# The opening of every projection and MLP phase: the first weight slab in two halves, and PE's first pass outside its loop

## The reference

```python
for l in range(DEPTH):                      # 4 layers
    kind, j = l % N_MIXERS, l // N_MIXERS
    hp, hs = modulate(xp, mp[0], mp[1]), modulate(xs, ms[0], ms[1])
    if kind == 0:                           # layers 0 and 3: RWKV-7
        ...  # r, k, v = xr @ w_rkv[0], xk @ w_rkv[1], xv @ w_rkv[2]; scan; y @ w_o
    elif kind == 1:                         # layer 1: attention
        ...  # qkv = h @ w_qkv; attention; @ w_o
    else:                                   # layer 2: gated DeltaNet
        ...  # proj = h @ w_in; chunked delta rule; @ w_o
    xp = deepnorm_residual(xp, dp, mp[2], ln_g[l, 0], ln_b[l, 0])
    xs = deepnorm_residual(xs, ds, ms[2], ln_g[l, 0], ln_b[l, 0])
    # squared_relu_mlp(h, w_fc1, w_fc2) = square(relu(h @ w_fc1)) @ w_fc2, D_FF = 4096
    xp = deepnorm_residual(xp, squared_relu_mlp(modulate(xp, mp[3], mp[4]), w_fc1[l], w_fc2[l]), mp[5], ...)
    xs = deepnorm_residual(xs, squared_relu_mlp(modulate(xs, ms[3], ms[4]), w_fc1[l], w_fc2[l]), ms[5], ...)
```

## Time and profile before

| | |
|---|---|
| time, median of 3 runs | 6409.85 us (6405.69 to 6411.26) |
| time of the profiled execution | 6404.79 us |
| its span | 6402.7 us |
| PE busy | 5409.3 us (84%) in 66124 matmuls |
| DVE busy | 2506.2 us (39%) |
| ACT busy | 1872.1 us (29%) |
| DMA | 424.21 MB, a mean of 66 GB/s |

### The profile page before, as it was taken

How to read it: one execution, slowest core, us unless ns; L and a number is a source line. 1 busy time by engine, 2 the same in 40 slices (tenths; PEclk the granted TensorE clock), 3 DMA queues, 4 the chain that set the end, 5 groups by cost and what they waited for, 6 DMA issues and landing times. The chain is left out here.

```text
span 6402.7 us, 149362 instructions
## 1 busy us (share of the span) xinstructions
PE 5409.3 (84%) x66124; PEld 4859.5 (76%) x66124; DVE 2506.2 (39%) x4363; ACT 1872.1 (29%) x3847; POOL 586.3 (9%) x1076
## 2 busy tenths in 40 slices
PE   6678999978997487789978588789968899996998
PEld 2377888868996365689977577679948688885998
DVE  0233555434333522243331454343352355444433
ACT  1023334322222122322232343232222344333222
POOL 0002223200000000000000222000000232210000
PEclk8788999989998677899989799899989899997999
DMA  9621000012212100122122211122112100001221
GB/s 407 259 99 49 22 24 22 9 48 84 74 52 73 45 11 21 47 79 79 52 94 78 65 39 40 56 73 73 67 41 92 34 14 24 23 8 71 73 79 49
DMA packets 105057, 424.21 MB, mean 66 GB/s; under 512 B 19081, under 2 KB 34697, under 8 KB 73929
## 3 DMA queue, kind: packets, MB, share of 16 engines
q1 hardware_dynamic: 91280, 386.14, 17.1%
q10 hardware_dynamic: 13248, 30.15, 1.2%
HBM read 367.25 MB, written 49.26 MB: 65 GB/s over the span
## 5 line engine op out<-in xcount | busy, mean ns | idle before, releaser
L356 PE MATMUL bank<-src_hi,ring_hi 128*128 128x320 f32 x4032 | 937.1, 314 | 344.6 <-DVE ring_lo L348 336.0
L356 PEld LDWEIGHTS bank<-src_hi,ring_hi 128*128 128x128 f32 x4032 | 686.6, 192 | 343.6 <-issue 339.2
L356 PE MATMUL bank<-src_lo,ring_hi 128*128 128x320 f32 x4032 | 933.2, 313 | 0.0
L356 PE MATMUL bank<-src_hi,ring_lo 128*128 128x320 f32 x4032 | 931.0, 313 | 0.0
L356 PEld LDWEIGHTS bank<-src_lo,ring_hi 128*128 128x128 f32 x4032 | 687.2, 191 | 5.4 <-issue 5.4
L356 PEld LDWEIGHTS bank<-src_hi,ring_lo 128*128 128x128 f32 x4032 | 685.8, 191 | 0.0
L348 DVE TENSOR_TENSOR ring_lo<-ring,ring_hi 128x2048 fp32r<-128x2048 f32 x190 | 434.9, 2289 | 513.9 <-ACT ring_hi L344 513.0
L562 ACT ACTIVATE stage<-bank 128x320 f32<-128x320 f32 x512 | 196.1, 435 | 1409.4 <-PE bank L356 1409.4
L356 PE MATMUL bank<-hidden_hi,ring_hi 128*128 128x320 f32 x2048 | 467.2, 309 | 0.0
L356 PE MATMUL bank<-hidden_lo,ring_hi 128*128 128x320 f32 x2048 | 467.1, 309 | 0.0
L356 PE MATMUL bank<-hidden_hi,ring_lo 128*128 128x320 f32 x2048 | 467.0, 309 | 0.0
(11 more groups left out here) (361 smaller groups left out, 8673.2 us busy)
## 6 DMA issues: line engine op xcount, KB each, us to landing
ring<-w_mlp SPq DMA_DIRECT2D x128, 1024.0 KB, 4.8
mod_ring<-w_mod SPq DMA_DIRECT2D x48, 2048.0 KB, 12.1
ring<-rw_wrkv SPq DMA_DIRECT2D x24, 1024.0 KB, 4.9
ring<-dn_win SPq DMA_DIRECT2D x16, 1024.0 KB, 5.1
rkv<-stage ACTq DMA_DIRECT2D x48, 320.0 KB, 2.2
r_k<-rkv SPq DMA_DIRECT2D x32, 320.0 KB, 3.6
src<-mixed SPq DMA_DIRECT2D x32, 320.0 KB, 8.0
dn_proj<-stage ACTq DMA_DIRECT2D x32, 320.0 KB, 2.2
```

Of the source, the lines that this page charges most:

```text
L356: last = self.nc.tensor.matmul(acc[h][:, 0:HALF], wt[:, n % 2, k, m * P:(m + 1) * P], x[:, k, h * HALF:(h + 1) * HALF], start=first and q ...
```

## The change

The first slab of each of the sixteen phases is loaded, cast and subtracted in two halves: FRONT, its blocks k 0 to 3, and BACK, its blocks k 4 to 7. FRONT has three semaphores of its own. SP issues FRONT ahead of everything; with `load` one source block follows, then BACK, then the other seven source blocks. ACT and DVE do the two halves at places of their own among the source blocks. PE waits for FRONT before product 0 and for BACK before product 4. For these waits PE's pass 0 is written out ahead of the loop, which then runs from pass 1.

```diff
+    def load_first(self, sp, part):
+        done = self.s["w_half"] if part is FRONT else self.s["w_loaded"][0]
+        sp.dma_start(self.raw[:, 0, part].rearrange("p k n -> p (k n)"),
+                     slab(self.w, 0)[:, part.start * 2 * P:part.stop * 2 * P]).then_inc(done, 16)
+    def upper_first(self, act, part):
+        act.wait_ge(self.s["w_half"] if part is FRONT else self.s["w_loaded"][0], 16)
+        self.nc.scalar.copy(self.hi[:, 0, part], self.raw[:, 0, part]).then_inc(self.s["wh_half" if part is FRONT else "wh_ready"], 1)
...
 # projection, SP
+                ring.load_first(sp, FRONT)
                 if load is not None:
-                    for b in range(NB):
+                    sp.dma_start(src[:, 0, :], load[0]).then_inc(s["src_loaded"][0], 16)
+                ring.load_first(sp, BACK)
+                if load is not None:
+                    for b in range(1, NB):
                         sp.dma_start(src[:, b, :], load[b]).then_inc(s["src_loaded"][b], 16)
-                        if b == 1:
-                            ring.load(sp, 0, PER, 0)
-                else:
-                    ring.load(sp, 0, PER, 0)
                 ring.load(sp, 0, PER, 1)
 # projection, PE
-                with pe.Fori(0, n_pass) as i:
+                def block_(i, first):
                     for n in range(PER):
-                        pe.wait_ge(s["wl_ready"], at(i, PER, n + 3))
+                        if n or not first:
+                            pe.wait_ge(s["wl_ready"], at(i, PER, n + 3))
...
-                                if u == 0:
+                                if first and u == 0:
                                     pe.wait_ge(s["src_ready"], k + 1)
+                                    if k == FRONT.start:
+                                        pe.wait_ge(s["wl_half"], 1)
+                                    if k == BACK.start:
+                                        pe.wait_ge(s["wl_ready"], 3)
...
+                block_(0, True)
+                with pe.Fori(1, n_pass) as i:
+                    block_(i, False)
 # projection, ACT
+                    if load is not None and b == 0:
+                        ring.upper_first(act, FRONT)
...
-                    if b == 2:
-                        ring.upper(act, 0, PER, 0)
+                    if load is None and b == 2:
+                        ring.upper_first(act, FRONT)
+                    if b == (3 if load is None else 0):
+                        ring.upper_first(act, BACK)
 # projection, DVE
+                    if load is not None and b < 2:
+                        ring.rest_first(dve, (FRONT, BACK)[b])
...
-                    if b == 3:
-                        ring.rest(dve, 0, PER, 0)
+                    if load is None and b in (2, 3):
+                        ring.rest_first(dve, (FRONT, BACK)[b - 2])
 # mlp, ACT and DVE (SP and PE as above)
-                    if b == 2:
-                        ring.upper(act, 0, PER, 0)
+                    if b in (3, 4):
+                        ring.upper_first(act, (FRONT, BACK)[b - 3])
...
-                    if b == 3:
-                        ring.rest(dve, 0, PER, 0)
+                    if b in (3, 4):
+                        ring.rest_first(dve, (FRONT, BACK)[b - 3])
```

More of the change, by code:

```diff
@@ L312, in _ @@
             modulate_blocks(dve, nc, g, lambda b: None, mod_at(0, 1), mod_at(0, 0))
-SPLIT_SEMS = ["w_loaded:2", "wh_ready", "wl_ready", "mm_done", "evacuated", "hi_ready", "src_ready"]
+SPLIT_SEMS = ["w_loaded:2", "wh_ready", "wl_ready", "mm_done", "evacuated", "hi_ready", "src_ready", "w_half", "wh_half", "wl_half"]
+FRONT, BACK = slice(0, NB // 2), slice(NB // 2, NB)
 HALF = T // 2
@@ L338, in load, with rest_first @@
                      slab(self.w, i * per + n)).then_inc(self.s["w_loaded"][n % 2], 16)
+    def load_first(self, sp, part):
[5 more added lines that the diff above has]
+        self.nc.scalar.copy(self.hi[:, 0, part], self.raw[:, 0, part]).then_inc(self.s["wh_half" if part is FRONT else "wh_ready"], 1)
+    def rest_first(self, dve, part):
+        dve.wait_ge(self.s["wh_half" if part is FRONT else "wh_ready"], 1)
+        self.nc.vector.tensor_tensor(self.lo[:, 0, part], self.raw[:, 0, part], self.hi[:, 0, part].bitcast(F32),
+                                     ALU.subtract).then_inc(self.s["wl_half" if part is FRONT else "wl_ready"], 1)
     def upper(self, act, i, per, n):
@@ L516, in _ @@
             def _(sp):
-                with sp.Fori(0, QUARTERS) as i:
+                ring.load_first(sp, FRONT)
+                ring.load_first(sp, BACK)
+                for n in range(1, PER):
+                    ring.load(sp, 0, PER, n)
+                with sp.Fori(1, QUARTERS) as i:
                     for n in range(PER):
@@ L523, in _, with block_ @@
                 pe.sem_inc(s["mm_done"], 4)
-                with pe.Fori(0, QUARTERS) as i:
+                def block_(i, first):
                     for n in range(PER):
-                        pe.wait_ge(s["wl_ready"], at(i, PER, n + 3))
+                        if n or not first:
+                            pe.wait_ge(s["wl_ready"], at(i, PER, n + 3))
                         for m in range(2):
@@ L538, in _ @@
                             last.then_inc(s["mm_done"], 1)
+                block_(0, True)
+                with pe.Fori(1, QUARTERS) as i:
+                    block_(i, False)
             @block.scalar
```

## The result

The kernel after takes 6362.23 us (median of 4 runs, 6355.86 to 6366.58) against 6410.56 us before (4 runs beside them, 6405.69 to 6414.69). The ratio is 0.9925, with a 95% interval from 0.9913 to 0.9937: 48 us faster. The forecast was 6349, with a range from 6337 to 6372. The direction was right and the time inside the range, but 13 us above the middle, and a fifth of the expected gain did not come. The profiled execution took 6355.86 us, its span 6354.1 us against 6402.7.

The account below looks back on a forecast made before the run. PE bounds the projection and MLP phases, latency the rest. Gains of 28.6 + 28 - 4 + 8.6 - 0.4 = 60.8 us, taken from 6409.85, gave 6349 us, range 6337 to 6372.

Parts of the forecast that it names:

- Source in SBUF: `at_wqkv`, `dn_win` and four `mlp`: PE starts 4.7 or 4.8 us earlier and the phases keep it; 28.6 us together.
- Source by DMA: Four output products: unit 0's product 7 ends 7.3 us sooner in layer 0, 6.6 to 7.5 elsewhere; sum 28 us.
- clock rival: Where PE now pauses in unit 0, ten openings: clock stays at 0.50 longer, costing 20 to 28 us; 6372; chance 0.10.
- Source made by DVE: Six products with `mix`: PE starts sooner, but unit 0 waits for DVE's longer chain; a loss of 4 us.
- PE's pass outside the loop: The written-out first pass costs nothing itself but moves PE's loops; 8.6 us won in the third `mlp`, at 85%.
- the step on the third loop: Third `mlp`: its loop body moves 17 places, out of the bad ones, ending 8.6 us of branch stalls; 85%.
- The rival's 6355: Third `mlp` still misses, at two branches, giving back two thirds of 8.6 us; chance 0.10 together with all four missing.
- the prediction's two signs of being wrong: Granted clock in unit 0 stays at 0.50 beyond 7 us, or third `mlp`'s fetches continue after its loop's first pass.
- halves land together: A half takes a slab's 4.8 us: FRONT 1.2 us later in twelve openings, gain 15 us smaller; 6364; chance 0.06.
- The slower rival: All 16 openings: clock doesn't rise before unit 1 is through, 95 us lost less the 61; 6444; chance 0.02.

Follow-up runs that it names:

- The run with the 64 waits: The kernel after with 64 already-met PE waits ahead of the third `mlp`'s loop, moving it 32 places; 6341.92 us, ratio 0.9896.
- the kernel with 434 waits: The kernel after with 434 already-met PE waits ahead of the first `mlp`'s loop, moving every later PE instruction 217 places; one run, 6396.86 us.

## Why the prediction was right, and where it was wrong

**Source in SBUF: right in the start, and lucky in the total.** The start comes 4.3 to 4.9 us sooner in the six phases (forecast 4.7 and 4.8). FRONT lands 4.1 us after its issue in `at_wqkv` and the first `mlp`, not 3.6, and a half takes ACT 1.04 and DVE 1.23 us, not 0.95 and 1.14. An estimate by the Trainium skill's page "DMA: Bandwidth & Descriptors", section "Anatomy of one DMA", is 3.2 us for this half; the Trainium skill gives that formula for transfers issued by GpSimd, and these are issued by SP. The trace has 0.9 more, and the measurement decides. The end of unit 0 gained 4.3 to 5.7 us. In four of the six it gained more than the start, by 0.4 to 1.3 us, where the low clock was shorter than before (3.1 us in `at_wqkv`, before 6.0). With the third `mlp`'s opening the six give 31.2 us against 28.6. The starts alone give 27.6. The other 3.6 came from the clock and are in no term of the sum, so it was luck for the forecast that they made good what other terms lacked.

**Source by DMA: mechanism right, 3.7 us over.** Of these 3.7, 2.6 are the long execution in the table; by the means (297.6 us over the three kernels with the old opening, 270.8 over the five with the new one) the gain is 26.7 of 28. The pause after product 0 came, 0.4 to 1.1 us long where 1.3 was forecast for layer 0. Two terms were mis-sized: FRONT landed 4.7 us after its issue in layer 0 and not 3.6, so the start was 7.9 us behind the first issue and not 6.8; and the clock, taken to rise as in a dense opening, stayed low for 8.0 to 9.3 us in three of four. This is the clock rival in a small form, in four openings and not in ten. With `mix` the pauses come later, and the low stretch was 3.2 to 5.9 us, within the 3.2 to 6.1 of the openings before (the prediction read them as 3.4 to 6.2).

**Source made by DVE: right.** Forecast -4, measured -3.8, by the steps given: PE starts earlier, DVE's chain is longer, and the pauses come from product 3 on. The whole slab in the kernel after, at 407.00 us, confirms the sign. It is also 2.9 us below the kernel before, where two slabs had landed late (the prediction has 5.6 and 6.4 us for them). That the size fits so closely is partly chance: three kernels with the old opening took 407.4 to 409.9 us, and by their mean, 408.6, the loss is 5.2.

**PE's pass outside the loop: the peel is free, but the step on the third loop failed.** The step said that the third body stood at most 20 places short of a good one, from the fourth body that was fine 20 places further on, and that 17 of the 20 take it out, at 85%. The edge lies behind 192, where the body stands now, and before 195, where the fourth stood. So the count and the bound were sound, and the case that was given 3 places of 20 came true. But its price was wrong. The rival's 6355 took the stalls to shrink by a third with the branches, from 8.6 to 5.7 us. They stayed at 8.2, as each of two branches stops PE for 4 us where each of three had cost 2.9, and two stretches at half clock came on top: 5.7 us of PE's work at 0.50 behind the first, half of it lost, and about as much behind the second. So this one loop holds 12.5 of the 13 us by which the forecast was too low; the other rows miss by little only because the clock's 3.6 us stand against the output products. The run with the 64 waits shows both parts together: 13.7 us. Of the prediction's two signs of being wrong both came true: 0.50 held beyond 7 us in three openings, and the third `mlp` went on fetching behind its first pass.

**The halves together; slower.** The rival "halves land together" fell: a half lands in 4.1 us in `at_wqkv`, and one transfer of the whole was cast 4.96 us after its issue. The slower rival needed 3.8 us lost in each opening. The longest stretch at the low level was 9.3 us against 6.2 in dense openings; 3.1 us more of it cost 1.4 us, a product taking 1.60 us and not 0.88.

## What to carry to other kernels

Split the first tile of a pipeline wherever the engine at its end has nothing to do until the whole tile is through; some 70% of the gain at the end of unit 0 came with the halved casts and subtractions here, and the rest with the halved transfer. But look at each place by itself. Where another engine's chain sets the end of the first unit, an earlier start only inserts waits, and where the consumer starts and then pauses it can pay with clock, so order the inputs such that it runs dense once it has started. A change that alters the length of an engine's program moves every loop behind it, so look at each branch back, before and after, and count what such a loop gives or takes apart from the change.

## What the hardware did that was not expected

- A loop of 1,564 PE instructions branches back in 0.21 to 0.24 us or in 3.3 to 3.9 us, by where its body starts modulo 256: at seven places seen between 173 and 192 it stalled, at 153, from 195 to 251 and at 1 it did not. 64 waits that do nothing made the third `mlp` 13.7 us shorter.
- One such stall in one piece (3.9 and 4.2 us of idle PE) was followed by 5.7 us at a granted 0.50. Around the branch shown of the kernel before, where the idle time came in two pieces of 1.17 and 1.93 us, the clock stayed at 1.00. That two pieces are not always enough is seen in the second `mlp` of the kernel with 434 waits: pieces of 0.92, 2.76, 1.28 and 2.17 us, 7.1 in all, and a phase 14.4 us longer than in the kernel after.
- A pause of 0.1 to 1.1 us behind the first product of an opening went with up to 9.3 us at the low clock, against at most 6.2 without it, but not every time. What decides between them in one opening stays open.
- With the source in SBUF and a dense start, the early openings (PE at 6.4 to 6.8 us behind the barrier, one at 8.1) came to the full clock within 4.0 us of the first matmul in 26 of 42. None of the 24 that started later, at 7.3 to 11.5 us, did.
